# A third of the adaLN product as VectorE dots over transposed weight slabs, and contiguous weight slabs everywhere

## The reference, cut to what matters

```python
def trunk_layer(x, cond, w_ada, b_ada, g1, g2, w_in, ...):
    sh1, sc1, gt1, sh2, sc2, gt2 = split(silu(cond) @ w_ada + b_ada, 6)   # adaLN: (1024) @ (1024 x 6144)
    h = rmsnorm(x, g1) * (1.0 + sc1) + sh1
    aq, ai, aff, afb, ag, bq, bk, bv, ga, gb = split_columns(h @ w_in)
    o_a = hgrn2_mixer(...); o_b = attention(...)
    y = (sigmoid(ga) * (o_a @ w_oa) + sigmoid(gb) * (o_b @ w_ob)) @ w_out
    x = x + gt1 * y
    h2 = rmsnorm(x, g2) * (1.0 + sc2) + sh2
    x = x + gt2 * peer(h2, p_wq, p_keys, p_u, p_v)     # 128 expert rows gathered per token
```

## Time and profile before

| | before |
|---|---|
| times of three runs | 2793.64, 2802.36, 2805.5 us |
| median | 2802.36 us |
| the profiled execution's own time | 2788.1 us |
| its span, first to last instruction | 2786.3 us |
| TensorE busy | 2135.5 us, 77% |
| VectorE busy | 1707.8 us, 61% |
| ScalarE busy | 974.6 us, 35% |
| GpSimd busy | 858.0 us, 31% |

### The profile page before, as it was taken

How to read it: one execution, slowest core, us unless ns; L and a number is a source line. 1 busy time by engine, 2 the same in 40 slices (tenths; PEclk the granted TensorE clock), 3 DMA queues, 4 the chain that set the end, 5 groups by cost and what they waited for, 6 DMA issues and landing times.

```text
span 2786.3 us, 28232 instructions
## 1 busy us (share of the span) xinstructions
PE 2135.5 (77%) x6941; PEld 1156.3 (42%) x6941; DVE 1707.8 (61%) x4192; ACT 974.6 (35%) x2506; POOL 858.0 (31%) x797
## 2 busy tenths in 40 slices
PE   8787897865558599968957877777877877767777
PEld 3386844655546454554522332332332322323222
DVE  2123167765556756743377777677777776776775
ACT  0312134240035444222134444343443443443433
POOL 0010022532311112100034444444543444434444
PEclk9898998977866789978978999888888999989999
DMA  8663778760023267733369999999999999999998
GB/s 282 196 198 114 234 262 300 265 227 16 1 95 121 104 240 277 254 127 125 127 262 418 406 404 422 377 387 420 385 410 374 396 420 405 410 377 379 397 406 336
DMA packets 201681, 790.95 MB, mean 284 GB/s; under 512 B 12772, under 2 KB 116582, under 8 KB 119622
## 3 DMA queue, kind: packets, MB, share of 16 engines
q0 software_dynamic: 92464, 672.05, 60.7%
q1 hardware_dynamic: 107368, 112.40, 12.3%
q10 hardware_dynamic: 1712, 4.98, 0.5%
HBM read 786.10 MB, written 3.28 MB: 283 GB/s over the span
## 4 chain that ended last, share of the span: by engine, by line
PE 33%; DVE 23%; issue 19%; DMA 14%; POOL 5%; ACT 4%; DVEq 1%; POOLq 0%; ACTq 0%; SPq 0%
PE pa L531 24%; DMA RG<-in_uv,idxs 10%; PE pl L507 4%; DVE PB L1133 3%; DVE PB L1115 2%; DMA HL<-in_uv,idxs 2%; DVE R L1174 2%; DVE PB L1113 2%; DVE pl L1191 2%; PE po L531 2%; PE pa L534 2%; POOL HG L1031 2%; DVE PB L1143 1%; DVE PB L1145 1%; DVE PB L1146 1%
## 5 line engine op out<-in xcount | busy, mean ns | idle before, releaser
L1016 POOL DMA_INDIRECT RG<-in_uv,idxs x288 | 310.8, 1079 | 807.0 <-DVE pl L1191 475.0
L507 PE MATMUL pl<-RING,PB 128*128 128x512 f32 x768 | 412.3, 679 | 167.5 <-ACT PB L829 167.5
L507 PE MATMUL pl<-RG,PB 128*128 128x512 f32 x768 | 376.6, 631 | 108.7 <-ACT PB L829 108.1
L819 ACT ACTIVATE agel<-apre 128x1 f32<-128x1 f32 x640 | 127.7, 200 | 900.7 <-DVE apre L1174 891.5
L1016 POOL DMA_INDIRECT RING<-in_uv,idxs x192 | 243.1, 1266 | 323.4 <-PE pl L507 290.8
L507 PEld LDWEIGHTS pl<-RING,PB 128*128 128x128 f32 x768 | 150.8, 208 | 423.2 <-ACT PB L829 273.5
L531 PE MATMUL pa<-HL,RING 128*128 128x512 f32 x704 | 308.2, 596 | 4.0 <-ACTq L372 4.0
L1174 DVE CUSTOM_DVE_ANT_0 R<-RING,AB 128x1024 f32<-128x1024 f32 x192 | 235.0, 1225 | 109.5 <-DMA RING<-in_uv,idxs 88.5
L1174 DVE CUSTOM_DVE_ANT_0 R<-RG,AB 128x1024 f32<-128x1024 f32 x192 | 229.9, 1225 | 110.7 <-DMA RG<-in_uv,idxs 74.5
L507 PEld LDWEIGHTS pl<-RG,PB 128*128 128x128 f32 x768 | 144.1, 197 | 327.3 <-ACT PB L829 183.1
L829 ACT ACTIVATE PB<-CT,wexp 128x128 f32<-128x128 f32 x512 | 205.6, 402 | 183.0 <-PE pl L507 152.1
(11 more groups left out here) (224 smaller groups left out, 2943.0 us busy)
## 6 DMA issues: line engine op xcount, KB each, us to landing
RING<-in_w_in SPq DMA_DIRECT2D x42, 1024.0 KB, 6.1
RING<-in_w_ada SPq DMA_DIRECT2D x24, 1024.0 KB, 5.2
RING<-in_w_pq SPq DMA_DIRECT2D x16, 1024.0 KB, 5.3
RING<-in_w_out SPq DMA_DIRECT2D x8, 1024.0 KB, 6.8
RG<-in_uv,idxs POOLq DMA_INDIRECT x288, 9.1
RING<-in_w_oa SPq DMA_DIRECT2D x8, 512.0 KB, 4.3
RING<-in_w_ob SPq DMA_DIRECT2D x8, 512.0 KB, 5.5
RING<-in_uv,idxs POOLq DMA_INDIRECT x192, 11.0
```

What stands on the lines that cost most here:

```text
L507: last = nc.tensor.matmul(PL[:, c * 512:(c + 1) * 512], DG[:, k % 2, :], bufs[k % len(bufs)][:, D + c * 512:D + (c + 1) * 512], start=Fals ...
L819: A(agel[:, par, k:k + 1], apre[:, par, k:k + 1], ACT.Gelu).then_inc(gel_done, 1)
L1016: nc.gpsimd.indirect_dma_start(out=bufs[b], out_offset=None, in_=uv, in_offset=bass.IndirectOffsetOnAxis(ap=idxs[:, par, k:k + 1], axis=0) ...
```

## The change

It has three parts.

1. **Slabs lie contiguously in memory.** The host arranges every weight so that each slab is one block in which each partition's 8 KB (9 KB for the routing weights with their keys) lie together. Each slab is one DMA. There is the same number of bytes. "wo" and "wpq" slabs, which were two DMAs, become one.
2. **Segments 3 and 4 leave TensorE.** `ADA_SEGS` = 1, 0, 2, 5: 16 slabs on TensorE. The 2048 columns of segments 3 and 4 come as eight transposed "col" slabs: a partition holds two whole columns of 1024 weights. VectorE multiplies each with the silu of the condition, spread over the partitions in `CONDB` (1 MB, a new load), and sums: four dots of 1024 elements for a slab (two columns, two conditions). The bias is added at the end.
3. **The order.** From TensorE's slab 10 on, col slabs lie in the ring between TensorE's slabs. All five sums of squares are taken after slab 5; the norms of tiles 2, 3 and 4 stand before the dots of col slabs 0, 1 and 2; the transposes of tile t follow slab 9 + t; ScalarE's scaling lies between its gate copies. The last two col slabs lie between the first winT slabs. Tile 0's projections wait only for tile 0, the wait for all five tiles stands before those of tiles 1 to 4.

The ring's order from its 11th entry on is: col 0, ada 10, col 1, ada 11, col 2, ada 12, col 3, ada 13, col 4, ada 14, col 5, ada 15, col 6, winT 0, col 7, winT 1, winT 2, ... The number of slots is still three.

```diff
-ADA_SEGS = [1, 0, 2, 3, 4, 5]
-NADA = 4 * len(ADA_SEGS)
+ADA_SEGS = [1, 0, 2, 5]
+NADA, NFIRST, NCOL, XT_FROM, COL_FROM = 16, 8, 8, 9, 10
...
+for _n in range(NADA):
+    SLABS += ([("col", _n - COL_FROM)] if _n >= COL_FROM else []) + [("ada", _n)]
+_turned = [("winT", w, m) for w in WIN_T for m in range(2)]
+for _n in range(NADA - COL_FROM, NCOL):
+    SLABS += [("col", _n), _turned.pop(0)]
+SLABS += _turned + [("win", w, a) for w, a in WIN]
...
@@ SyncE @@
-                if n >= NSLAB:
+                if n >= NSLAB and SLABS[n - NSLAB][0] == "col":
+                    sp.wait_ge(coldot_done, SLABS[n - NSLAB][1] + 1)
+                elif n >= NSLAB:
                     wait_full(sp, last_use(SLABS[n - NSLAB]))
...
+                sp.dma_start(at[:, 0:SLOTW if kind == "wpq" else SLAB], src).then_inc(s, 16)
                 if n == 2:
                     sp.dma_start(XP[:], x_prompt).then_inc(x_in, 16)
                     sp.dma_start(XL, x_sample.rearrange("(t p) d -> p t d", p=P)).then_inc(x_in, 16)
-                if n == NADA:
+                    sp.dma_start(CONDB, cond_rows.rearrange("p (c d) -> p c d", c=2)).then_inc(condb_in, 16)
+                if key == ("winT", W_Q, 1):
...
@@ TensorE @@
             for n in range(NADA + 1):
                 if n < NADA:
+                    ada_row(n)
+                if n:
+                    ada_mod(n - 1)
+                t = n - XT_FROM
+                if 0 <= t < NT:
+                    pe.wait_ge(xn_ready, t + 1)
+                    ps = start(("xT", t))
                     for k in range(KD):
+                        last = tr(ps[:, k * P:(k + 1) * P], XN1[:, t % 2, k * P:(k + 1) * P])
+                    finish(("xT", t), last)
+
+            pe.wait_ge(hT_ready, 1)
...
@@ VectorE @@
+            def col_dots(i):
+                slot, count = slab_turn[("col", i)]
+                dve.wait_ge(slab_in[slot], count)
+                for m in range(2):
+                    n = 2 * i + m
+                    for c in range(2):
+                        ins = V.tensor_tensor_reduce(out=CJUNK, in0=RW_[:, slot * SLOTW + m * D:slot * SLOTW + (m + 1) * D],
+                                                     in1=CONDB[:, c, :], scale=1.0, scalar=0.0, op0=ALU.mult, op1=ALU.add,
+                                                     accum_out=ADA[:, 2 + n // KD, c, n % KD:n % KD + 1])
...
+            for n in range(NFIRST + 1, NADA):
+                row(n)
+                if n >= COL_FROM:
+                    t = n - COL_FROM + 2
+                    if t < NT:
+                        wait_full(dve, ("xT", t - 2))
+                        normed(t, x0(t), XN1[:, t % 2, :])
+                    col_dots(n - COL_FROM)
+            for n in range(NADA - COL_FROM, NCOL):
+                col_dots(n)
```

More of the change, by code:

```diff
@@ L77 @@
 POOL_LEAD = 3
-SLABS = ([("ada", n) for n in range(NADA)]
-         + [("winT", w, m) for w in WIN_T for m in range(2)]
-         + [("win", w, a) for w, a in WIN])
+SLABS = []
+for _n in range(NADA):
[4 more added lines that the diff above has]
+SLABS += _turned + [("win", w, a) for w, a in WIN]
 for _b in range(len(BATCHES)):
@@ L133, in plan_groups @@
             names.append(("mod", n - 1))
-    names.extend(("xT", t) for t in range(NT))
+        if 0 <= n - XT_FROM < NT:
+            names.append(("xT", n - XT_FROM))
     names.extend(("winP", w, m) for w in WIN_T for m in range(4))
@@ L188, with build @@
 INDEX = {name: i for i, name in enumerate(NAMES)}
-def build(nc, x_prompt, x_sample, cols, rows, normf_rows, brow, consts, masks, sel, w_ada, w_in, w_oa, w_ob, w_out,
-          w_pq, keysT, uv, state, ckT, cv, y_prompt, y_sample, new_state, new_k, new_v):
+def build(nc, x_prompt, x_sample, cols, rows, normf_rows, brow, consts, masks, sel, cond_rows, ada_slabs, col_slabs, in_slabs, o_slabs,
+          out_slabs, pq_slabs, uv, state, ckT, cv, y_prompt, y_sample, new_state, new_k, new_v):
     with ExitStack() as ctx:
@@ L247, in build @@
         MK4 = view(AB, 4096, 15, P)
+        CONDB, CJUNK = view(AB, 768, 2, D), AB[:, 2816:2816 + D]
         XL = view(R1, 0, 4, D)
@@ L462, in _ @@
                 kind = key[0]
[L463 to L467, removed]
-                else:
[L469 to L481, removed]
+                if kind == "ada":
+                    src = ada_slabs[ADA_SEGS[key[1] // 4] * 4 + key[1] % 4]
+                elif kind == "col":
+                    src = col_slabs[key[1]]
+                elif kind in ("win", "winL", "winT", "winTL"):
+                    src = in_slabs[key[1] // SC_W + key[2]]
+                elif kind in ("gate_a", "gate_b"):
+                    src = in_slabs[(W_GA if kind == "gate_a" else W_GB) // SC_W + key[2]]
+                else:
+                    src = {"wo": o_slabs, "wout": out_slabs, "wpq": pq_slabs}[kind][key[2]]
+                sp.dma_start(at[:, 0:SLOTW if kind == "wpq" else SLAB], src).then_inc(s, 16)
                 if n == 2:
@@ L539, in _, with ada_row, ada_mod @@
             pe.wait_ge(cond_ready, 1)
+            def ada_row(n):
+                w = chunks(slab("ada", n))
+                ps = start(("ada", n))
+                for k in range(KD):
+                    last = mm(ps[0:2, 0:SC_W], condT[:, :, k], w[:, k, :], k == 0, k == KD - 1)
+                finish(("ada", n), last)
+            def ada_mod(n):
+                pe.wait_ge(grow_ready, n + 1)
+                ps = start(("mod", n))
+                row = GR[n % 2]
+                if ADA_SEGS[n // 4] in GATE_SEGS:
+                    for c in range(2):
+                        last = mm(ps[:, c * SC_W:(c + 1) * SC_W], SEL[:, c, :], row)
+                else:
+                    for m in range(2):
+                        last = nc.tensor.transpose(ps[:, 2 * m:2 * m + 2], row[:, m * P:(m + 1) * P], ident[0:2, 0:2])
+                finish(("mod", n), last)
@@ L540, in _ @@
             for n in range(NADA + 1):
                 if n < NADA:
-                    w = chunks(slab("ada", n))
-                    ps = start(("ada", n))
-                    for k in range(KD):
[L545 to L558, removed]
@@ L782, in _ @@
             post(0)
+            pe.wait_ge(hT_ready, NT)
             win_turned("winTL", "winT", hTl, LAT)
@@ L843, in _, with gate_rows @@
             step(A(LB[:, :, 2:4, :], LB[:, :, 0:2, :], ACT.Exp), lbe_ready)
-            for n in range(NADA):
+            act.wait_ge(condb_in, 16)
+            step(A(CONDB, CONDB, ACT.Silu), condb_ready)
+            def gate_rows(n):
                 s, c0 = ADA_SEGS[n // 4], (n % 4) * SC_W
[L847 to L854, removed]
+                ps = group(("mod", n))
+                if s == GATE_SEGS[0]:
+                    step(A(G1P[:, c0:c0 + SC_W], ps[:, 0:SC_W], ACT.Copy))
+                    step(A(G1L[:, c0:c0 + SC_W], ps[:, SC_W:2 * SC_W], ACT.Copy), *freed(("mod", n)), gate_ready)
+                else:
+                    step(A(G2[:, :, c0:c0 + SC_W], ps[:, 0:512].rearrange("p (c n) -> p c n", c=2), ACT.Copy),
+                         *freed(("mod", n)), gate_ready)
             def root(n):
@@ L872, in _ @@
                 root(t)
-            act.wait_ge(am_ready, 3)
-            for t in range(NT):
-                turned("xT", t, 0, hT_ready)
+            act.wait_ge(am_ready, 2)
+            for n in range(NFIRST, NADA):
+                gate_rows(n)
+                if n - NFIRST < NT:
+                    turned("xT", n - NFIRST, 0, hT_ready)
             WT = ((W_Q, QU, ACT.Silu, q_ready), (W_FF, lambda u: FU(0, u), ACT.Sigmoid, sig_ready),
@@ L1235, in row, with scale_col @@
                      *freed(("ada", n)), grow_ready)
+            def scale_col(which, col, at):
+                for c in range(2):
+                    step(V.scalar_tensor_tensor(AM[:, which, c, :], ADA[:, at, c, :], 1.0, CO[:, col:col + 8],
+                                                ALU.add, ALU.mult))
+                dve.sem_inc(am_ready, 1)
+            def col_dots(i):
+                slot, count = slab_turn[("col", i)]
+                dve.wait_ge(slab_in[slot], count)
+                for m in range(2):
+                    n = 2 * i + m
+                    for c in range(2):
+                        ins = V.tensor_tensor_reduce(out=CJUNK, in0=RW_[:, slot * SLOTW + m * D:slot * SLOTW + (m + 1) * D],
+                                                     in1=CONDB[:, c, :], scale=1.0, scalar=0.0, op0=ALU.mult, op1=ALU.add,
+                                                     accum_out=ADA[:, 2 + n // KD, c, n % KD:n % KD + 1])
+                        if m and c:
+                            step(ins, coldot_done)
+                        else:
+                            step(ins)
@@ L1237, in _ @@
             row(0)
-            for n in range(NADA):
-                if n + 1 < NADA:
-                    row(n + 1)
+            for n in range(NFIRST):
+                row(n + 1)
```

(22 more changed lines are left out.)

14 lines of the change are left out of this document (10 added, 4 removed).

## The result

The changed kernel takes 2829.18 us in the median of four runs (2823.87 to 2834.59) beside 2801.34 us before (2793.64 to 2805.5). The ratio is 1.0111, 95% interval 1.0092 to 1.013: slower by 1.1%. The profiled execution took 2831.4 us, its span is 2829.6.

What follows compares the result with a forecast made beforehand. DMA engines bound the kernel from the 21st slice on (0.96 busy); in the first 138 us TensorE is the chain. Projections ending 27 us later, less 2 us behind them, make +25: 2802.4 becomes 2827 us, range 2802 to 2847.

Steps and rivals of the forecast that it cites:

- The lockstep: In the shared ring of three slots, load, TensorE's slab, VectorE's row and dots run in series, five turns of 16.9 us.
- A turn, 16.9 us: One ring round: reaction 0.1, load 4.7, TensorE 5.6, row and hand-overs 0.8, four dots 5.7 us; bounds 13.7 and 20.9.
- The start: Up to the first dots: CONDB's extra 1.05 MB delays slab 3 from 26.1 to 28.8 us; col 0 done at 70.3.
- The way back to a fed TensorE: After the turns: winT 0 computed by 167.0 us, winT 2 landing at 174.2, tile 0's projections ending at 213.0.
- The 56 us that the change alone would give: Before the projections: 30 us of TensorE slabs gone and 26 us moved between the slabs, taken alone 56 us off.
- measuring point: End of tile 0's projections, 185.75 us before, forecast 213.0; what the change does there it does to the end.
- Behind the measuring point, -2 us: After tile 0's projections: contiguous slabs shorten VectorE's waits for gathers by 2 us; bounds 0 and 12.
- The clock: TensorE's slab in each turn: after idling some 9 us it starts at half clock, 5.6 us instead of 3.55.
- No lockstep: Rival for the ring: dots and TensorE's slabs overlap, a turn costs 7 us, total 2779 us; chance 0.07.
- Short turns: Rival for the ring: lockstep, but turns of 13.7 to 14.9 us, total about 2814 us; chance 0.12.
- Contiguity wins later: Rival for 353 to 1400 us: contiguous weights save 12 us where they meet gathers, total about 2815 us; chance 0.08.

Runs made afterwards that it cites:

- e2: Changed kernel with each col slab's dots placed ahead of the row of TensorE's slab in VectorE's program, from slab 10 on; 2774.25 us, ratio to before 0.9933.
- e3: Changed kernel with the eight col slabs loaded into three slots of their own, the ring of three serving TensorE's slabs alone; 2768.35 us, ratio to before 0.9892.
- e6: Changed kernel with two of the four dots of each col slab left out; 2807.02 us, ratio to before 1.0043.
- e8: The changed kernel measured once more, unaltered, beside the same runs of before; 2820.89 us, ratio to before 1.0088.
- e1: Kernel before with only the contiguous slabs, one load each, and all 24 adaLN slabs on TensorE; 2792.87 us, ratio to before 0.9996.
- e5: Changed kernel's new order and contiguous slabs, but all 24 adaLN slabs kept on TensorE, without dots or condition rows; 2781.65 us, ratio to before 0.9950.
- e7: Changed kernel with col slabs in own slots, dots spread between rows, sums of squares one by one, masks, states and rows loaded later; 2754.42 us, ratio 0.9861.
- e9: Changed kernel with 22 or 23 unread matmuls a turn added on TensorE while it waits for the next slab; 2816.14 us, ratio to before 1.0080.
- e4: Changed kernel with 16 or 18 unread matmuls a turn added on TensorE while it waits for the next slab; 2824.3 us, ratio to before 1.0108.

## Why the prediction was right

The forecast was 2827 us, the median came out at 2829.18. Point by point:

- **The lockstep.** Right, and shown: e2 removes VectorE's half of it, e3 the ring's half (with three slots more), and each makes the kernel faster than before; e6 shows that the parts add.
- **A turn, 16.9 us.** Turns without a norm took 16.24, 16.54 and 16.8 us. The load was 4.84 us from issue to landing (4.7 assumed); TensorE's slab 5.86 (5.6); row and hand-overs 0.7 (0.8); four dots with the release 5.12 (5.7). The dots were sized too high: behind a dot the next started after 0.04 us, not after the 0.18 that I took from a dot behind an instruction of another kind. The dots' error and those of load and TensorE cancelled in part; five turns took 85.3 us where 86.5 stood.
- **The start.** Sized wrong: slab 3 started at 25.38 us (26.28 in e8), not at 28.8. The extra megabyte was paid (e1 and e5, without it, start slab 3 at 23.73 and 23.47), but it came on top of loads that were faster than before's: the first slab ran 1.6 us earlier. Slab 9 then took 5.30 us instead of 3.55, at a granted clock of 0.50 from 52 to 54 us. This term wasn't in the sum and gave part of the gain back; the first dots ended at 68.33 instead of 70.3.
- **The way back to a fed TensorE.** winT 0 at 158.87 (161.6), winT 2 at 172.46 (174.2), end at 211.2 (213.0).
- **The 56 us that the change alone would give.** No run reached them. Part 3 alone gives 22 us at the measuring point (e5); without lockstep and with early columns it was 45.6 us (e7).
- **Behind the measuring point, -2 us.** Not borne out: the waits for gathers didn't shrink (50.1 us in e1, 44.2 before).
- **The clock.** That TensorE starts a turn's slab at the lower clock was right: all five took 5.4 to 6.2 us. The argument for it, that every idle time over 4 us ends at 0.50, doesn't hold: in the earlier trace rows transposes run at 1.10 us behind an idle 4.01 us, and the granted clock there, from 307 to 312.2 us, is 1.00. The idle times of 8.6 to 10 us in the turns all ended at 0.50; for shorter ones see the last section.
- **The rivals.** "No lockstep" was named with 2779 us, 23 under before; e2, which makes it so in half, is 20 under the before beside it. "Short turns" stood at 2814, 12 us over before. e9 comes nearest to its case, and is 22 us over its before: its turns without a norm were 15.1 and 14.7 us long, above the rival's 14.9 in one of two, and its measuring point is 19 us late. "Contiguity wins later" with its 12 us is refuted by e1.
- **Chance in it.** The profiled before lay 14 us under its median, the profiled after 2 us over its own. The sum was made to the span and carried over. The two profiles of the changed kernel end their projections at 211.2 and 216.2 us, with the forecast's 213.0 between them, and the two comparisons give +28 and +25 us. So the mechanism and the sum are confirmed to some 5 us; that the median came out within 2 us of the forecast is luck.

## What to carry to other kernels

When two consumers share a ring of buffers, write down for each load which use frees its slot, and beside it each consumer's program order; if one waits in it for the other's next item before it frees its own, buffers and engines run in series, whatever share of the work was moved. Here less work (e6) shortened the series and left it one, and one swap in a program (e2), or slots of its own for each consumer (e3), took it apart. Moving work off the busiest engine pays only once the waits between its pieces are out: with the lockstep the moved third cost 0.9 to 1.1%, while the better order without it gave 0.5% (e5), with own slots 1.1% (e3), and with the dots spread out as well 1.4% (e7).

## What the runs showed of the hardware

Loads of 1 MB in pieces of 8 KB were hardly faster than in pieces of 1 KB: between 33 and 100 us they took 4.9 us in the median in e1 against 5.2 before from issue to landing, and 0.33 against 0.37 us for the issue itself. The kernel as a whole gained nothing from it that can be measured (0.9996).

An idle time of 2.2 us can be followed by TensorE's lower clock. In the changed kernel's timeline slab 9 starts 0.2 us after a wait of 2.24 us and takes 5.30 us for what takes 3.55 at full clock. The granted clock is still 1.00 during the wait (47.7 to 50 us) and 0.50 from 52 to 54 us, when TensorE is at work again:

```profile
50.02 0.28 PE L558 MATMUL pa<-CT,AB 2*128 2x2 f32 x2 [2.24 <-DVEq L379]
...
50.23 5.30 PE L533 MATMUL pa<-RING,condT 128*2 128x256 f32 x16
```

The length of the wait alone doesn't tell. In e5 the same wait of 2.24 us at the same place left the clock up: slab 9 took 3.62 us, at a granted clock of 1.00. So did a wait of 2.08 us ahead of slab 3 in before and one of 3.08 us ahead of slab 3 in e7, while in e4 the clock came down behind 2.80 us. All idle times of 8.6 to 10 us in the changed kernel's turns ended at the lower clock.
